# One-core block kernel: where dots, routing pieces and pair weights stand among the second half's dense steps

## The reference

```python
sc = jnp.einsum("bshpd,hpnd->bshpn", qp, sub_keys)        # 8 heads, 2 x 128 keys
s1, i1 = lax.top_k(sc[..., 0, :], 16); s2, i2 = lax.top_k(sc[..., 1, :], 16)
cand = s1[..., :, None] + s2[..., None, :]                # 16 x 16 sums
top_s, top_c = lax.top_k(cand, 16)
expert = e1 * N_KEYS + e2; gate = softmax(top_s)
w = gate * gelu(einsum(h, peer_u[expert]))                # dots
y = einsum(w, peer_v[expert])                             # combine
```

## Time and profile before

| | us |
|---|---|
| median of 3 runs | 2665.09 |
| lowest, highest | 2660.74, 2676.69 |
| the profiled execution: its own time | 2649.01 |
| its span, first to last instruction | 2647.2 |
| second half's dense part, with the first half's experts | about 905 to 1962 |
| of it band attention | about 968 to 1021 |
| memory attention | about 1250 to 1270 |
| latent norms, turns, latent and forget attention | about 1632 to 1840 |
| tail: the second half's experts alone | about 1962 to 2647 |

### The profile page before, as it was taken

How to read it: one execution, slowest core, us unless ns; L and a number is a source line. 1 busy time by engine, 2 the same in 40 slices (tenths; PEclk the granted TensorE clock), 3 DMA queues, 4 the chain that set the end, 5 groups by cost and what they waited for, 6 DMA issues and landing times.

```text
span 2647.2 us, 27076 instructions
## 1 busy us (share of the span) xinstructions
PE 2051.6 (77%) x9586; PEld 1426.0 (54%) x9586; DVE 1377.2 (52%) x3083; ACT 459.9 (17%) x1127; POOL 1078.8 (41%) x1090
## 2 busy tenths in 40 slices
PE   8898989999989988997999999788772333333334
PEld 6787778887476766775677775345460000000001
DVE  4435331002423886556665455844368667676751
ACT  2311131001342222112211012333120000000000
POOL 2011000000000445554555454455267777767775
PEclk9899989998968989998899989878996665566557
DMA  7368414443404989997999999877699999999998
GB/s 260 136 242 289 136 56 151 151 151 104 141 30 151 382 317 337 389 401 294 338 379 393 371 385 334 313 256 289 244 370 392 410 409 409 408 379 403 410 409 355
DMA packets 214728, 779.19 MB, mean 294 GB/s; under 512 B 23891, under 2 KB 26515, under 8 KB 213571
## 3 DMA queue, kind: packets, MB, share of 16 engines
q0 software_dynamic: 155136, 564.97, 55.3%
q1 hardware_dynamic: 57272, 207.44, 22.1%
q10 hardware_dynamic: 2187, 5.05, 0.5%
HBM read 770.78 MB, written 6.58 MB: 294 GB/s over the span
## 4 chain that ended last, share of the span: by engine, by line
PE 58%; DMA 13%; DVE 11%; POOL 9%; issue 7%; ACT 2%; ACTq 0%; POOLq 0%; DVEq 0%; SPq 0%
PE bank L577 42%; DMA main<-in_peer_u,idx 10%; POOL main L513 9%; PE bank L762 5%; DVE main L1562 3%; PE bank L658 2%; PE bank L698 2%; PE bank L716 2%; DMA main<-in_peer_v,idx_v 2%; PE bank L707 1%; DMA ring<-in_w_stream 1%; PE bank L667 1%; PE bank L1026 1%; DVE main L1441 0%; ACT main L1058 0%
## 5 line engine op out<-in xcount | busy, mean ns | idle before, releaser
L577 PE MATMUL bank<-main,ring 128*128 128x256 f32 x4864 | 1070.5, 381 | 19.6 <-DVE main L1731 10.6
L577 PEld LDWEIGHTS bank<-main,ring 128*128 128x128 f32 x4864 | 921.4, 191 | 177.9 <-issue 30.7
L513 POOL DMA_INDIRECT main<-in_peer_v,idx_v x512 | 522.5, 1021 | 480.2 <-PE bank L762 344.1
L762 PE MATMUL bank<-main,w_wide 128*32 128x512 f32 x2048 | 369.2, 857 | 389.1 <-DMA main<-in_peer_v,idx_v 364.3
L513 POOL DMA_INDIRECT main<-in_peer_u,idx x512 | 519.0, 1014 | 310.4 <-issue 124.1
L1562 DVE CUSTOM_DVE_ANT_0 main<-h_a,main 128x1024 f32<-128x1024 f32 x256 | 313.9, 1226 | 200.1 <-DMA main<-in_peer_u,idx 193.9
L762 PEld LDWEIGHTS bank<-main,w_wide 128*32 128x32 f32 x2048 | 73.0, 137 | 618.3 <-issue 617.2
L1562 DVE CUSTOM_DVE_ANT_0 main<-bank,main 128x1024 f32<-128x1024 f32 x224 | 274.2, 1224 | 167.8 <-issue 152.6
L1058 ACT ACTIVATE main<-bank 128x256 f32<-128x256 f32 (+5 forms) x344 | 144.6, 438 | 758.1 <-PE bank L577 714.8
L577 PE MATMUL bank<-ring,main 128*128 128x512 f32 (+3 forms) x624 | 236.3, 538 | 18.6 <-DMA ring<-in_w_stream 9.6
L577 PEld LDWEIGHTS bank<-ring,main 128*128 128x128 f32 x624 | 111.9, 197 | 136.8 <-issue 119.8
(11 more groups left out here) (226 smaller groups left out, 1450.7 us busy)
## 6 DMA issues: line engine op xcount, KB each, us to landing
ring<-in_w_stream SPq DMA_DIRECT2D x370, 512.0 KB, 5.8
main<-in_w_ada POOLq DMA_DIRECT2D x48, 512.0 KB, 6.9
main<-in_peer_u,idx POOLq DMA_INDIRECT x512, 8.5
main<-in_peer_v,idx_v POOLq DMA_INDIRECT x512, 8.7
main<-in_sub_keys SPq DMA_DIRECT2D x2, 1024.0 KB, 8.4
main<-rows_d SPq DMA_DIRECT2D x1, 1536.0 KB, 8.6
main<-in_xT ACTq DMA_DIRECT2D x1, 1024.0 KB, 5.1
main<-in_memT POOLq DMA_DIRECT2D x1, 1024.0 KB, 8.8
```

The costliest lines, as they stand in the source:

```text
L513: gp.indirect_dma_start(rows_buf[:, slot, :], None, table, bass.IndirectOffsetOnAxis(ap=where, axis=0)).then_inc(landed[slot], 16)
L577: ins = pe.matmul(o, lhsT, rhs, **kw)
L762: last = mm(y_bank[half][s * CG:(s + 1) * CG, :], w_wide[:, lo:lo + CG], (v_rows, u_rows)[second][:, slot, half * 512:(half + 1) * 512], s ...
```

## The change

- In the attentions, the latent projections, the head norms and the turns, DVE's `until` emits the experts' steps due 10 us before the stage's modelled time, instead of those due by that time. Other points are unshifted.
- `weigh(k - 1)` stands behind the fifth dot of a pair (j == 4), not the seventh.
- `route` yields once less: the one-hot's product, its sum and the index are one piece.
- On PE `turn_idx` is due EARLY = 4 us later and `turn_w` 1 us later; on ACT `gelu` is due 12 us behind a pair's last dot, not 3, and a pair's first `widen` 6 us later.

```diff
@@ PE, experts()
-                            yield math.inf if ends_half else pace.batch(b + q) - 1.0
+                            yield math.inf if ends_half else pace.batch(b + q) + EARLY - 1.0
                             turn_idx(k + 1)
                         if q == PER_PAIR - 1 and k + 1 < NT * PAIRS:
-                            yield pace.batch(b + q) - 1.0
+                            yield pace.batch(b + q)
                             turn_w(k + 1)
@@ ACT, experts()
-                    yield pace.dot(PAIR * k + PAIR - 1) + 3.0
+                    yield pace.dot(PAIR * k + PAIR - 1) + 12.0
                     gelu(k)
-                    yield pace.batch(b - 1) if b % (TH * CG) else pace.batch(b) - 6.0
+                    yield pace.batch(b - 1) + 6.0 if b % (TH * CG) else pace.batch(b) - 6.0
                     widen(PH * k)
@@ DVE, route()
                 st(ve.tensor_tensor(oh, oh, per_entry(top_i[:, :]), ALU.mult))
-                yield
                 st(ve.reduce_sum(e_f, onehot[:, :].rearrange("p (k i) -> p k i", i=TOPK), axis=AX_X))
@@ DVE, experts()
-                        if j == 6 and k > k0:
+                        if j == 4 and k > k0:
                             weigh(k - 1)
@@ DVE
+            BEHIND = dict.fromkeys(("band", "mem", "lat", "fox_qk", "turn", "mla", "fturn", "fox"), 10.0)
+
             def until(hf, stage, part=0.0):
                 if hf:
-                    experts_now.until(pace.at(hf, stage, part))
+                    experts_now.until(pace.at(hf, stage, part) - BEHIND.get(stage, 0.0))
```

## The result

The kernel after takes 2645.8 us (median of 7, 2638.0 to 2650.12) where the kernel before, run beside it, takes 2665.39 (7 runs): ratio 0.9919, 95% interval 0.9895 to 0.9943. Forecast were 2649 us, 2628 to 2677, and "within 1%" as the likeliest case; all three hold. The profiled execution took 2638.93 us (span 2637.1), 10.1 us less than that of before; the medians lie 19.6 apart. The profiled execution of the kernel before (2649.01 us) was 16 us under its median, that of the kernel after 7 us. So what follows from the two traces accounts for 10.1 us, and the rest of the 19.6 is seen in no trace.

The account below looks back on a forecast made before the run. The prediction took VectorE as the chain in the second half's attentions and turns, with a fixed DMA-bound tail. Terms summed to -18.5 us, less 2.5 given back: -16, from 2665.1 to 2649 us, range 2628 to 2677.

Parts of the forecast that it names:

- rival A: Second half's attentions: TensorE's clock returns with the waits removed, saving 12 us more, to 2637 us; chance 0.18.
- Latent norms, -4.1: Ahead of the first latent head norm: three dots and a routing wait leave, cutting TensorE's 8.79 us wait by 4.1.
- Third latent score, -3.6: Before the third latent score: routing pieces go behind it, one dot comes in, so TensorE's 7.36 us wait loses 3.6.
- Latent attention, +1.0 (0 to +3.6): Between latent attention's units: pieces add 3.6 us of VectorE work, mostly hidden behind TensorE; cost +1.0 us.
- The term for the later gelu and `widen`, 0 (-2 to +2): ScalarE's queue: later gelu and widening end its standing there, but TensorE isn't held by that; 0 us.
- Forget attention, -4.3: Before the third forget score: VectorE's dots, numbered three gathers earlier, start sooner, so TensorE's 4.28 us wait goes.
- Band, -6.5: Band attention: one dot leaves its entry (-1.3 us), and the L1480 waits of 4.2 and 1.0 us go.
- Memory attention, +1.5 (0 to +3.8): Memory attention: one-hot and one more dot come in, 3.8 us against 1.9 us of VectorE idle; cost +1.5 us.
- Weights two dots sooner, -2.5: At L744, the turn of a pair's weights: two dots leave the place ahead, cutting the 9.4 us wait by 2.5.
- Give-back, +2.5: After 1020 us: TensorE comes sooner to peer_v rows, for which it waited 14.2 us, so 2.5 us are returned.
- rival B: Second half's attentions: gathers pace them, waits return on peer_v at L762, gain about 3 us, to 2662; chance 0.14.
- Rival C, late dots: Latent norms: late dots hold gathers and combines once VectorE lags over 21 us; net +43, to 2708 us; chance 0.08.

Follow-up runs that it names:

- behind_gelu: The kernel before with the stages' 10 us and ScalarE's due times; weights, two-piece one-hot and TensorE's list as before: 0.9951 of the kernel before.
- old_list: The kernel after with TensorE's turned indices and turned weights due as in the kernel before: 0.9942 of the kernel before.
- old_weights: The kernel after with a pair's weights made at dot 6 again: 0.9960 of the kernel before.
- old_both: The kernel after with both TensorE's old list of turns and the weights at dot 6 again: 0.9917 of the kernel before.
- after_again: The kernel after, unchanged, run once more on another chip: 0.9934 of the kernel before there.
- no_mem: The kernel after with the memory attention taken out of the stages read 10 us earlier: 0.9982 of the kernel before.
- gelu_only: The kernel before with only ScalarE's later due times for gelu and first widening: 0.9979 of the kernel before.
- no_behind: The kernel after with the stages' 10 us set to 0, its other edits kept: 1.0020 of the kernel before.
- gelu_again: The kernel before with only ScalarE's later due times, run once more on another chip: 0.9992 of the kernel before.
- before_fill: The kernel before with 40 and 20 unused matmuls ahead of TensorE's waits for the third latent and third forget score: 1.0009 of the kernel before.
- before_again: The kernel before, unchanged, traced once more on the chip of the last set of experiments: 2754.3 us.

## Why the prediction was right, point by point

The number was right, and its steps only in part. The forecast gain and the one in the traces, block by block (us, each rounded; the third latent score and the latent attention are one block):

```
              band  to mem  mem  to latent latent forget to dense end   sum
forecast      -6.5   -2.5  +1.5    -4.1     -2.6   -4.3     +2.5      -16.0
measured      -3.7   -0.7  +3.8    -0.8     -9.6   -9.1     +2.5      -17.5
```

The blocks outside the latent and the forget attention were to give 9.1 us and gave 1.2 the other way; these two were to give 6.9 and gave 18.7, most of it at a higher clock, which the forecast left to rival A. That the two errors cancel to 1.5 us is luck, and so is part of the agreement with the median, of whose 19.6 us the traces hold 10.1. The range had a slip too: its upper bound of +16 would give 2681, not 2677.

- *What bounds it.* The "issue" share of 22.4% was misread: the chain's "issue" pieces of 1.1 us lie where a dot runs, and between two dots are only some 0.04 us. The reading that VectorE is the chain there stands. The tail was said to be of fixed length, so that the dense part's end decides. It holds: 687.2 to 691.7 us in six kernels whose dense end differs by 15 us (chip A and the chip of the result, which is of its kind), 751.0 to 756.6 in eight on chips B and C.
- *Latent norms, -4.1.* Right at its place: 8.79 to 4.73, and 4.7 in every kernel with the stages' 10 us but behind_gelu (3.80), 8.5 to 8.8 in every one without. But the block from memory to latent attention is only 0.8 us shorter; 3.3 us came back as small waits, L577 behind DVE L1754 (2.3 for 1.0 us) among them. The step "what leaves a block is caught up behind it at nothing" fell here.
- *Third latent score, -3.6.* Failed. The term took DVE as the chain without a pause from the head norms to the score. Once three dots had gone from ahead of them, DVE ran into ScalarE's squares (L1285), which need TensorE's last projection:

```profile
1697.10 1.22 DVE L1810 TENSOR_REDUCE small<-main 128x16 f32<-128x1024 f32 x1 [3.05 <-ACT main L1285]
```

  From the first head norm to the first attention unit VectorE took 53.91 us for 54.26, with these 3.05 in it: they are nearly all of the 3.6 that did not come. TensorE's wait is 7.52 us here and in old_list, old_weights and old_both, 7.55 in after_again. On chip B it did fall, to 2.75 us in behind_gelu and 1.10 in no_mem, but TensorE then waited 4.6 and 5.5 us in the transposes just ahead of the first score (1.3 in the kernel after), so that the wait had mostly moved. Work taken from an engine gains only up to its next wait, and that one had to be looked for in the rows ahead of the fourth norm.
- *Latent attention, +1.0 (0 to +3.6).* The block was 9.6 us shorter, with the failed wait inside. The stages' 10 us, for which the term was made, may well cost what it says (2.9 us from gelu_only to behind_gelu, in single executions); what shortens the block comes with the other edits (57.5 us in no_behind). The gelu that stood in it, with two table loads,

```profile
1728.30 1.28 ACT L1116 ACT_TABLE_LOAD   x1
1729.60 0.23 ACT L1116 ACTIVATE dots<-dots 128x32 f32<-128x32 f32 x1
1729.85 1.28 ACT L1087 ACT_TABLE_LOAD   x1
```

  (kernel before) cost TensorE 1.78 us and behind it the clock. The term for the later gelu and `widen`, 0 (-2 to +2), looked at queues alone; this is the mis-sized term: gelu_again has 7.6 us in this block from this edit. That other edits take part is open.
- *Forget attention, -4.3.* Its wait went (4.28 to 0.56; -3.7), and the block shrank by 9.1 us: the rest goes with the clock, 0.96 for 0.82 in its rows.
- *Band, -6.5.* It gave 3.7 in the result's pair (49.5 for 53.2), more beside other kernels (8.3 on chip B, where gelu_only's band of 57.9 us is the longest of all). The entry gave 1.2 of 1.3; of the 4.23 at L1480 1.93 stayed.
- *Memory attention, +1.5 (0 to +3.8).* At its bound: 24.4 for 20.6 us, and 4.9 more in behind_gelu than in gelu_only. Waits of 2.39 us at its third score and 2.09 at L1480 are the pieces that came in.
- *Weights two dots sooner, -2.5.* Right at its wait: 9.4 to 6.86. The block gave only 0.7 us in the result's pair; on chip A it is 3 to 5 us longer without the edit. That it, the list or the one-hot costs where gathers are slower was not foreseen.
- *Give-back, +2.5.* TensorE's waits for peer_v rows stayed (13.4 for 14.2 us); rival B did not come. The tail's +4.5 in this pair is in the scatter of tails.
- *Rival A, 0.18, 2637 us.* What it describes is what the trace of the result shows, with 16.3 us in two attentions where it was given 12 in three; its time, 2637 us, is 9 us under the measured one, since the terms outside these attentions came short. The Trainium skill, "TensorE: Matmul & The Clock Gate", section "HAM oscillation — how this bites in real kernels", has a wait between bursts slow the next burst: the trace agrees at the long waits (1.65 us for a pair behind 7.36 and 7.52 us, 0.81 where before_fill works in place of the wait) and behind the 1.78 us (2.02, and 1.08 where the wait is 1.01). It doesn't at every short one: behind one and the same wait of 1.58 us the products start slow in the kernel before and fast in the kernel after.

```profile
1746.82 1.70 PE L716 MATMUL bank<-main 128*128 128x64 f32 x8 [1.58 <-DVE main L1480]
```
```profile
1743.78 1.07 PE L716 MATMUL bank<-main 128*128 128x64 f32 x8 [1.58 <-DVE main L1480]
```

  The gain was larger than the waits removed in the latent and the forget attention, and not in the band (3.7 us for 1.2 and 2.3).
- *Rival C, late dots.* POOL's waits for dots rose from 10.5 to 17.9 us between 1632 and 1710, those for L762 fell from 26.5 to 14.3: its sign is there, its decision point was not reached. A shift of more than 10 us was not tried.

What carries the gain, then: on chip B a part of it is the stages' 10 us (behind_gelu under gelu_only by 0.28%) and a part ScalarE's due times (0.21%). On chip A the gain is in what old_both keeps, these two and the one-hot, and how it divides is open, since neither gelu_only, no_behind nor the fill ran there. That the latent and the forget attention gain together with the clock is what the result's trace shows (16.3 of 18.7 us). That the clock is the cause is argued and not shown: before_fill saved 14.3 us of matmul time and no time, and no_behind, without the 10 us, has nearly the low busy time of the kernel after in the two attentions (100.3 us; 116.7 in gelu_only) and gains nothing over the whole. No version was found that beats the kernel after beyond the measurement; old_both (0.9917 for 0.9934) is as good.

## What to carry to other kernels

Where engines take turns, look at the whole block behind a removed wait, and at the clock that its matmuls get; and before counting the gain, ask which wait the relieved engine meets next (3.05 us of 3.6 here). Judge an edit by the sum of the blocks up to the next fixed point, not by the block it stands in: before_fill won 11.5 us in one attention and kept 1.0 behind the next. Before a difference of single traces is explained, see how far the same block scatters in kernels that are alike there (3 us here). A two-piece operation on a shared scratch tile is safe only as long as nothing may be ordered between the pieces, so such an edit belongs to the reordering and not to the time.

## What the runs showed of the hardware

- Chips differ by 3% on one program: 2664 us on one, 2752 and 2754 us on others. Between the traces of the kernel before (spans 2647.2 and 2751.7 us), some 65 of the 104.5 us lie in the tail, where only rows are gathered (tails of 687 to 692 us at 395 to 400 GB/s, 751 to 757 at 364 to 369), and most of the rest in the second half's dense part. A gain of 0.4 to 0.8% on one need not be there on another: the new weights, list and one-hot seem to be such a case.
- Two table loads of 1.28 us around a 0.23 us gelu in the latent attention leave TensorE idle for 1.78 us, and matmuls of 1.08 us take 2.02 behind it. Without them there the block was 7.6 us shorter in one pair of executions, and the program not measurably (0.9992).
- The same 590 or so matmuls of two attentions took from 98.3 us of TensorE's time (the kernel after) to 120.6 (before_again); the mean granted clock was 0.89 and 0.73. Work of 14.5 us in place of two waits brought the clock of the latent attention from 0.70 to 0.92 and its own matmul time down by 14.3 us, and the two attentions together became 1.0 us shorter.
